# Four reorderings in a two-layer streaming-encoder trunk: value products, an attention block, a modulation tile, and the buffers of the down projection's last chunks

## Time and profile before

| what | us |
|---|---|
| median of 3 runs | 1456.1 (1455.23 to 1457.14) |
| the profiled execution, its own time | 1454.87 |
| its span, first to last instruction | 1453.0 |
| TensorE matmuls busy | 1366.1 (94%) |
| VectorE busy | 774.2 (53%) |
| ScalarE busy | 510.5 (35%) |
| GpSimd busy | 541.4 (37%) |
| TensorE's mean granted clock | 0.958 |

### The profile page before, as it was taken

The page is one execution under the profiler, slowest core; times in us unless marked ns, Lnnn a source line. Parts: engine busy times, 40 slices in busy tenths (PEclk is TensorE's granted clock), DMA queues, the critical chain, the costliest instruction groups (busy, mean ns, idle before and its releaser), DMA issues. The chain is left out here.

```text
span 1453.0 us, 17110 instructions
## 1 busy us (share of the span) xinstructions
PE 1366.1 (94%) x6812; PEld 1019.3 (70%) x6812; DVE 774.2 (53%) x1370; ACT 510.5 (35%) x778; POOL 541.4 (37%) x328
## 2 busy tenths in 40 slices
PE   5989899998999999899899999999899999989986
PEld 2546676776888888688655576767688888868865
DVE  5885767645667666532368646574533333321125
ACT  2523134435433333322233422253443333332322
POOL 0630100565544444344446110055744444434432
PEclk9999999898999999899999999999999999999988
DMA  9345733021665555454314451002133232322321
GB/s 384 137 116 164 155 107 117 16 87 41 212 191 180 187 192 191 139 195 153 119 60 117 78 72 45 30 30 73 44 102 101 87 102 88 101 72 88 97 63 58
DMA packets 64798, 166.76 MB, mean 115 GB/s; under 512 B 14288, under 2 KB 26960, under 8 KB 64208
## 3 DMA queue, kind: packets, MB, share of 16 engines
q1 hardware_dynamic: 64720, 165.68, 36.8%
HBM read 160.04 MB, written 5.62 MB: 114 GB/s over the span
## 5 line engine op out<-in xcount | busy, mean ns | idle before, releaser
L2044 POOL TENSOR_TENSOR ring_r<-ring,scr_r 128x1024 fp32r<-128x1024 f32 x148 | 360.2, 2435 | 441.0 <-ACT scr_r L1913 273.6
L442 PE MATMUL bank<-ym_r,scr_r 128*128 128x512 f32 x704 | 280.7, 399 | 5.3 <-DVE hm_r L1565 4.7
L444 PE MATMUL bank<-hm_r,scr_r 128*128 128x512 f32 x704 | 280.0, 398 | 0.0
L443 PE MATMUL bank<-ym_r,ring_r 128*128 128x512 f32 x704 | 277.2, 394 | 0.0
L442 PE MATMUL bank<-scr_r 128*128 128x512 f32 x480 | 197.5, 411 | 25.3 <-issue 14.2
L443 PE MATMUL bank<-scr_r,ring_r 128*128 128x512 f32 x480 | 191.0, 398 | 0.0
L1581 DVE SCALAR_TENSOR_TENSOR scr<-bank,pb,scr 128x511 f32<-128x511 f32 x88 | 66.0, 750 | 212.7 <-ACT scr L1906 212.6
L512 PE MATMUL bank<-hm,ring 128*128 128x512 f32 x352 | 168.3, 620 | 0.0
L1067 DVE SCALAR_TENSOR_TENSOR ada<-ada,silu_c 128x1024 f32<-128x1024 f32 x80 | 135.0, 1690 | 50.1 <-DMA ada<-in_w_ada 50.1
L442 PEld LDWEIGHTS bank<-ym_r,scr_r 128*128 128x128 f32 x704 | 132.7, 189 | 38.2 <-issue 6.3
L444 PEld LDWEIGHTS bank<-hm_r,scr_r 128*128 128x128 f32 x704 | 132.6, 188 | 33.2
(11 more groups left out here) (324 smaller groups left out, 1795.8 us busy)
## 6 DMA issues: line engine op xcount, KB each, us to landing
ring<-in_w_up SPq DMA_DIRECT2D x88, 512.0 KB, 3.6
ada<-in_w_ada SPq DMA_DIRECT2D x80, 512.0 KB, 3.6
ring<-in_w_down SPq DMA_DIRECT2D x44, 512.0 KB, 3.5
ring<-in_w_in SPq DMA_DIRECT2D x34, 512.0 KB, 4.5
scr<-in_w_ada SPq DMA_DIRECT2D x16, 512.0 KB, 14.3
ring<-in_w_out SPq DMA_DIRECT2D x16, 512.0 KB, 3.6
pa<-in_par_a SPq DMA_DIRECT2D x2, 2144.5 KB, 12.9
xa<-in_x SPq DMA_DIRECT2D x1, 2048.0 KB, 8.1
```

What stands on the lines that cost most here:

```text
L442: first = mm(dst, w_hi, x_hi, start=start, stop=False)
L443: mm(dst, w_lo, x_hi, start=False, stop=False)
L444: return first, mm(dst, w_hi, x_lo, start=False, stop=stop)
L2044: G.tensor_tensor(ring_r[:, at, :], ring[:, at, :], high[:, at, :].bitcast(F32), ALU.subtract)\
```

## The change

Four edits; no arithmetic is changed. (1) TensorE runs the second third of projection U1 before the value products instead of after them, and its last third before the first attention block instead of after it. (2) VectorE runs attention block 6 before the second half of the S5 inputs instead of after it. (3) VectorE takes modulation tile 23 after the second diagonal copy instead of before the S5 gate product. (4) Inner tile 19 of the down projection gets the third pair of `ht`, so it no longer waits for a pair of `hs`.

```diff
         def inner(k):
-            if k < KF - TAIL + 2:
+            if k < KF - TAIL + 1:
                 return hs[:, k % 2, :], hs[:, 2 + k % 2, :]
-            t = k - (KF - TAIL + 2)
+            t = k - (KF - TAIL + 1)
             return ht[:, 2 * t, :], ht[:, 2 * t + 1, :]
...
                 k_heads()
+                project(AT[U1], 1)
                 v_blocks()
-                project(AT[U1], 1)
+                project(AT[U1], 2)
                 attend(0)
-                project(AT[U1], 2)
                 s5_turn(0)
                 attend(1)
...
-                s5_in(1)
                 operand(0)
                 attend(6)
+                s5_in(1)
                 mods_mix(8)
                 attend(7)
...
                 take(12)
-                mods_mix(23)
-
                 v.wait_ge(S["s5_gate"], l + 1)
...
                     ins.then_inc(S["s5_done"], 1)
                 take(13)
+                mods_mix(23)
                 v.wait_ge(S["gm_mm"], l + 1)
...
                 def inner_high(k):
-                    if 2 <= k < KF - TAIL + 2:
+                    if 2 <= k < KF - TAIL + 1:
                         a.wait_ge(S["down_mm"], l * (KF - TAIL) + k - 1)
```

## The result

The changed kernel took 1440.54 us in the median of six runs (1438.73 to 1442.39), the kernel before on the same chip 1455.66 (1449.86 to 1459.57). The ratio is 0.9891, 95% interval 0.9872 to 0.9909: of 1456 us that is 15.9 us (13.2 to 18.6). The forecast was 11.7 us, 1444.4 us. The sign is right, but more was won than the sum said. Two later comparisons of the same two kernels gave 0.9898 and 0.9903, so 14.1 to 15.9 us. The profiled execution took 1442.01 us, with a span of 1440.1 and a mean granted clock of 0.966 (before: 1453.0 and 0.958).

What follows compares the result with a forecast made beforehand. TensorE, busy in 94% of the span, was taken to bound the kernel. Terms 1.0 + 7.4 + 3.3 + 0.0 = 11.7 us took the median from 1456.1 to 1444.4 us; the 8-in-10 range was 1440.0 to 1449.5.

Steps and rivals of the forecast that it cites:

- Edit 2: Block 6 amid the S5 inputs: 5.7 us in layer 0 plus 1.7 in layer 1, 7.4; bounds 6.0 and 8.5.
- No wait came at `hg_turn`: After the second S5 input: no new wait was forecast at `hg_turn`; one standing there would show the prediction wrong.
- Edit 4: Down projection's end: 0.0 us in both layers, as chunk 21's load binds; below -1.7, above +0.5 per layer.
- Rival (b): Down projection's end: chunk 21 not bound by its load, up to 6 of 9.0 us won, 1438 us; chance 0.05.
- Edit 1: Value products: 1.7 in layer 0 plus 1.0 in layer 1, less 1.7 for falls: 1.0 us; bounds 2.7 and -1.6.
- the 1.7 taken off: New gap before Q0's second third: half a chance per layer of a 1.7 us clock fall, 1.7 us in all.
- Edit 3: Second join, layer 0 only: tile 23 moved away wins 3.3 us; bounds 1.5 and 4.8.
- 4.1 - 0.8: Layer 0 to the fifth output slice: 2.1 us wait plus 2.0 clock, less 0.8 for a likely later fall.
- The lower term of 2.2 us: Tile 23's new place: by the shared SBUF port it doubles or holds back GpSimd's pair sum; 2.2 us, total 10.6.
- rival (a): New waits at the edits cost more clock than charged: only 5 to 8 us won, 1448 to 1451; chance 0.17.

Runs made afterwards that it cites:

- the filled gap: The changed kernel with two products whose result nobody reads ahead of the attention block of turn 2: 0.9891 of the kernel before.
- none, join filled: The kernel before with products nobody reads put ahead of the second join, six in layer 0 and one in layer 1: ratio 1.0003.
- all, tail of three: The changed kernel with the last three chunks of the down projection run bank by bank instead of four: 0.9822 of the kernel before, 1429.3 us.
- all, tail of two: The changed kernel with the last two chunks of the down projection run bank by bank instead of four: 0.9813 of the kernel before, 1429.69 us.

## Why the prediction was right and wrong

Between the same instructions, the profiles of all these kernels can be laid over that of before. Worked out from TensorE's starts, in us against before's first profile (negative is shorter). The stretches are 103.8 to 144.3, 144.3 to 183.0, 183.0 to 270.4 and 270.4 to 347.2 of layer 0, then 808.6 to 847.9 and 847.9 to 862.4 of layer 1, in before's times:

```
edits in it      edit 1   edit 2   edit 3   behind   edit 1   edit 2
                 L0       L0       L0       it       L1       L1
none, again      -1.16     0.05    -0.01    -0.11    -0.01    -0.10
4                -0.27     0.13     0.29     2.81     0.00     0.17
1                -1.67     0.05     0.30     2.74    -0.92    -0.15
2                -1.68    -6.65     0.13    -0.25     0.03    -1.72
3                -1.19    -0.14    -3.47     0.05    -0.01     1.84
1, 2, 4          -1.68    -5.23    -0.63     2.56    -0.91    -1.73
2, 3, 4           0.45    -6.71    -3.46     0.99    -0.01    -1.72
1, 2, 3          -1.68    -5.31    -3.46     0.55    -0.91    -1.72
all              -1.69    -5.37    -3.47     0.55    -0.91    -1.73
all, again       -3.38    -5.94    -3.46    -2.15    -0.91    -1.73
all, third       -3.38    -5.26    -3.48     0.39    -0.90    -1.73
```

**Edit 2, right.** 5.2 to 5.9 in layer 0 wherever edit 1 is there too, 5.7 forecast; 1.7 in layer 1, 1.7 forecast. The wait for VectorE at the first state update is there, 1.0 to 1.7 us, but only with edit 1. Without it (edit 2 alone; edits 2, 3 and 4) it is 0.3, and TensorE keeps 6.7. In those two the second S5 input starts 9.2 us behind TensorE's S5 input products, with edit 1 9.9 to 10.6, behind GpSimd's first half, which waits for SP's DMAs. Why it is later with edit 1, no run isolates; the prediction had this bound in layer 0 whatever edit 1 does. No wait came at `hg_turn`.

**Edit 4, right**, for the reason given: the load of chunk 21 binds, and the chain shows it before and after. The down projection's end is neither shorter nor longer. Rival (b) is out.

**Edit 1, waits right, clock wrong.** The waits came where they were forecast, and layer 1 won 0.91 us in every kernel of the table with the edit, 1.0 forecast. The 1.7 of layer 0 holds only against before's first profile. From the value products to the first transpose it is 13.2 us in all nine profiles with edit 1 (the filled gap and the two tail kernels among them). Without it, it is 14.95 in that first profile and 13.2 to 14.7 in six others, 14.0 in the mean of the seven, so 0.8 is won. And what is won there is not the wait but a fall behind it. The value products took 3.78 us behind the old wait in the earlier trace rows, 2.00 in the changed kernel, and 2.00 as well with edit 2 alone, where the wait stayed, no fall followed, and the transpose came after the same 13.2. The prediction charged falls behind new waits and didn't look for the one behind the old.

Granted clock of four stretches of layer 0, in each profile, by the same windows. The first holds the value products, the second edit 1's new waits and what follows them, the third the end of the S5 kernels' products, the fourth the wait that edit 2 removes:

```
edits in it               102:112  112:124  130:138  156:166
none                       0.66     1.00     0.79     0.66
none, again                0.83     1.00     0.79     0.66
none, join filled          0.83     1.00     0.79     0.66
4                          0.66     1.00     0.79     0.66
3                          0.83     1.00     0.79     0.66
2                          1.00     1.00     0.79     1.00
2, 3, 4                    0.83     1.00     0.60     1.00
1                          1.00     1.00     0.79     0.67
1, 2, 4                    1.00     1.00     0.79     1.00
1, 2, 3                    1.00     0.86     1.00     1.00
all                        1.00     0.86     1.00     1.00
all, again                 1.00     1.00     1.00     1.00
all, third                 1.00     1.00     1.00     1.00
all, gap filled            1.00     1.00     0.79     1.00
all, tail of three         1.00     1.00     1.00     1.00
all, tail of two           1.00     1.00     0.79     1.00
```

Without edit 1 the clock is low at the value products in six profiles of seven, and behind the S5 kernels in all seven. With it, the first fall is gone in all nine; two have one in the new gap (0.86; six products in 4.44 us), four others have the one behind the S5 kernels, three have neither. So a fall did come behind the new waits at times, but never as one more. In layer 1 the value products took 3.11 us in before and 2.00 in the changed kernel, so there too a fall went (with edit 1 alone one is still there, and the stretch is 0.92 us shorter all the same). The fourth column is edit 2's, and the clearest: low in all six without it, full in all ten with it.

In the column's mean the kernels with edit 1 are at -2.2 (seven profiles, the filled gap's -1.67 among them) and those without at -0.7 (seven, before's first at 0 and the filled join's -1.17 among them). Edit 1 is worth about 1.4 + 0.9 = 2.3 us where I had 1.0. It is within the bounds; the error is the 1.7 taken off. Some luck is in how close the 2.7 without it comes: 1.7 at the transpose was 0.8, and falls that were saved later made up most of the difference.

**Edit 3, the same.** The join itself is 3.5 us earlier in all kernels with the edit (2.8 against the kernel with 1, 2 and 4). Behind it the executions scatter by up to 5 us, and by 3 among kernels with the same code there: by the granted clock of the windows from 264 to 284 us, TensorE is at 1.2 GHz there for none of it (the second profile with all edits) to 17 us (edit 4 alone). With edit 3 those six are at 0.1 on average, without it, before's first profile at 0 included, the six are at 1.3. So about 4.0 to 4.7 us, where I had 4.1 - 0.8. Of that the 2.8 to 3.5 at the join are solid; the 1.2 behind it is a difference of means of six within that scatter. The tile didn't double at its new place (1.20 us). In before it took 2.33 us beside GpSimd's remainders:

```profile
257.32 5.66 POOL L2044 TENSOR_TENSOR ring_r<-ring,scr_r 128x1024 fp32r<-128x1024 f32 x2 [7.08 <-ACT scr_r L1665]
```

The lower term of 2.2 us did not come true. The Trainium skill, SBUF — State Buffer, section "SBUF: two separate sides", says that of a VectorE instruction with two SBUF inputs and a GpSimd one that reads SBUF the one that starts second is blocked until the first is done. Beside the remainders the trace agrees (2.33 us for 1.22). Beside the pair sum it doesn't: that ran from 257.48, beside the tile from 257.31, and took 2.18 us, against 2.00 for the one before it:

```profile
255.22 2.00 POOL L2052 TENSOR_TENSOR hm<-hm 128x512 f32<-128x512 f32 x1
257.48 2.18 POOL L2052 TENSOR_TENSOR hm<-hm 128x512 f32<-128x512 f32 x1 [0.26 <-ACT hm L1860]
```

**The step that failed** is the one that took clock falls off twice: "I give each layer half a chance of a fall at 1.7 us" and "a fall later on, as likely as not, takes 1.7 back". Together 2.5 us. I counted each new gap as a fall added to those that before has. What the runs show is that before already has a fall behind the wait that edit 1 fills (3.78 us for 2.00; in six of seven profiles without the edit) and one behind the S5 kernels' products, that the first is gone in all nine profiles with edit 1, and that none of them has one more in its place. Over the whole kernel, too, there are fewer. In 68 executions of before the mean granted clock averages 0.9589; over some 1455 us that is 2 x 0.0411 x 1455 = 120 us at the 1.2 GHz level. In 17 of the changed kernel it is 0.9668, so 96 us. Without the two deductions the sum is 11.7 + 2.5 = 14.2, and the three comparisons gave 14.1, 14.8 and 15.9. By the stretches of the first table it is 2.3 + 7.1 + 4.0 to 4.7, so 13.4 to 14.1. For edit 1 the failure of the step is shown; for edit 3's 0.8 it lies within the scatter.

A second, smaller error: I carried the profiled execution's time over to the median by 1.2 us and took the terms from that one profile. Executions of before range from 1449.4 us at a mean clock of 0.965 to 1462.2 at 0.956, so one profile is good to some 3 us for everything that hangs on the clock. The range, which took in half of rival (a), looked the wrong way: rival (a) is the deduction made twice over, and the upside of having none was left to the bounds.

What stays open: why edit 3 alone measured 6.1 us. By its profile it is 3.5 at the join and 4.7 over the whole, within the interval of 3.8 to 8.4, and no run isolates a further cause. What decides where a fall lies, or whether one comes at all in the same code, was not settled either.

## What to carry to other kernels

Price a move by the wait in front of it and by what is late next; where the clock was alike both stood the test here, to 0.4 us. Look at the granted clock behind the old wait as well as behind the new one, and in several executions: don't charge a new short gap with a clock fall when the same stretch already has one. And where the last wait is for a load that can't come earlier, don't free buffers for it; put work ahead of it, as the tail of three chunks did for 11 us.

## What was not expected of the hardware

The clock falls behind the second join while TensorE is 100% busy in the record (4.00 of 4.00 us at 0.53), and full products ahead of it for 5.4 us didn't prevent it. How long a fall lasts, and whether it comes, differs between executions of one and the same code: in the three profiles of the changed kernel the mean from 264 to 284 us is 0.92, 1.00 and 0.93, and one has a fall at 117 us where the two others have none. TensorE from 264 to 284 us (columns as above), before, then edit 4 alone, which has this stretch unchanged:

```profile
264.00:284.00 20.00, 16.93 (x143) 15.87 (x142) 13.08 (x19) 6.73 (x11) 10.65 (x7) 0.74 0.04 6
```

```profile
264.00:284.00 20.00, 17.09 (x125) 16.25 (x125) 10.08 (x15) 6.73 (x11) 10.27 (x7) 0.57 0.00 1
```

A mean of 0.74 is 2 x 0.26 x 20 = 10 us at 1.2 GHz, one of 0.57 is 17.
